# Six heads' inverse in a decoder layer: three heads' transposed inverse and level products moved to the other half of the partitions

## The reference

```
sa    = einsum('bhvk,bhk->bhv', state, -kk_t)
state = state * w_t + sa * (kk_t * a_t) + v_t * k_t
out_t = einsum('bhvk,bhk->bhv', state, r_t)
```

## Time and profile before

| | |
|---|---|
| median of three runs | 1374.96 us |
| the profiled execution's own time | 1372.77 us |
| its span, first to last instruction | 1370.7 us |
| PE busy over the span | 1268.2 us (93%) |
| DVE busy over the span | 511.4 us (37%) |
| mean granted TensorE clock | 0.971 |
| first start of line 692 (batch 0) | 373.0 us |
| starts of line 692 in batches 1 to 7 | 407.5, 443.6, 478.5, 514.5, 550.3, 586.6, 622.9 us |
| last start of line 739 (batch 7) | 657.8 us |

### The profile page before, as it was taken

The page is one execution under the profiler, slowest core; times in us unless marked ns, Lnnn a source line. Parts: engine busy times, 40 slices in busy tenths (PEclk is TensorE's granted clock), DMA queues, the critical chain, the costliest instruction groups (busy, mean ns, idle before and its releaser), DMA issues.

```text
span 1370.7 us, 23143 instructions
## 1 busy us (share of the span) xinstructions
PE 1268.2 (93%) x9642; PEld 628.1 (46%) x9642; DVE 511.4 (37%) x934; ACT 349.3 (25%) x482; POOL 108.1 (8%) x177
## 2 busy tenths in 40 slices
PE   7999999999999999999999964999999999999960
PEld 3444444444577777777445532333333333333320
DVE  3035310344178887886355355111111111110118
ACT  1044302234134433345221112111111111111114
POOL 1000000000111111010000001011101010101010
PEclk9999999999999999999999986999999999999985
DMA  5110010010000000001704008866789499397135
GB/s 215 42 35 31 31 46 31 31 31 16 0 3 3 33 3 34 3 3 37 289 1 156 31 16 339 305 237 223 251 308 316 153 319 375 90 383 226 31 74 217
DMA packets 61012, 170.17 MB, mean 124 GB/s; under 512 B 3184, under 2 KB 3312, under 8 KB 60928
## 3 DMA queue, kind: packets, MB, share of 16 engines
q1 hardware_dynamic: 54384, 145.31, 28.2%
q0 software_dynamic: 6544, 23.63, 7.1%
HBM read 144.29 MB, written 24.64 MB: 123 GB/s over the span
## 4 chain that ended last, share of the span: by engine, by line
PE 86%; DVE 5%; ACT 4%; DMA 2%; issue 2%; SPq 0%; POOL 0%; POOLq 0%; DVEq 0%; ACTq 0%
PE PS L1762 32%; PE PS L204 19%; PE PS L1251 8%; PE PS L643 6%; PE PS L213 3%; PE PS L954 2%; PE PS L966 2%; PE PS L976 2%; PE PS L1755 2%; PE PS L347 1%; PE PS L1391 1%; PE PS L739 1%; DMA XS<-in_xT 1%; ACT XS L999 1%; PE PS L692 1%
## 5 line engine op out<-in xcount | busy, mean ns | idle before, releaser
L204 PE MATMUL PS<-XS 128*128 128x512 f32 x672 | 294.5, 598 | 7.3 <-DMA XS<-in_xT 6.9
L1762 PE MATMUL PS<-XS,YT 128*64 128x512 f32 x656 | 287.6, 596 | 0.9 <-DVE YT L1843 0.9
L1762 PE MATMUL PS<-SQ,YT 128*64 128x512 f32 x488 | 216.0, 596 | 0.0
L1762 PE MATMUL PS<-RK,YT 128*64 128x512 f32 x672 | 211.1, 593 | 0.0
L204 PEld LDWEIGHTS PS<-XS 128*128 128x128 f32 x672 | 127.2, 191 | 172.8 <-issue 164.0
L1762 PEld LDWEIGHTS PS<-XS,YT 128*64 128x64 f32 x656 | 89.0, 138 | 183.0 <-issue 181.9
L1850 DVE TENSOR_TENSOR YT<-YT,PS 128x256 f32<-128x256 f32 x42 | 15.8, 417 | 271.8 <-PE PS L1762 271.8
L1251 PE MATMUL PS<-SQ,YT 128*128 128x512 f32 x256 | 114.0, 594 | 0.0
L643 PE MATMUL PS<-XS 64*64 64x64 f32 x2880 | 101.2, 221 | 4.4 <-ACT XS L782 2.6
L1762 PEld LDWEIGHTS PS<-RK,YT 128*64 128x64 f32 x672 | 65.9, 137 | 74.8 <-issue 74.8
L643 PEld LDWEIGHTS PS<-XS 64*64 64x64 f32 x2880 | 90.2, 135 | 21.4 <-issue 13.1
(11 more groups left out here) (375 smaller groups left out, 1519.0 us busy)
## 6 DMA issues: line engine op xcount, KB each, us to landing
RK<-in_w_down SPq DMA_DIRECT2D x6, 2048.0 KB, 13.2
XS<-in_w_in SPq DMA_DIRECT2D x21, 512.0 KB, 3.2
XS<-in_w_gate SPq DMA_DIRECT2D x5, 2048.0 KB, 13.5
XS<-in_w_upx SPq DMA_DIRECT2D x5, 2048.0 KB, 18.9
XS<-in_w_down SPq DMA_DIRECT2D x5, 2048.0 KB, 10.2
RK<-in_w_gate SPq DMA_DIRECT2D x5, 2048.0 KB, 20.3
SQ<-in_w_gate SPq DMA_DIRECT2D x4, 2048.0 KB, 21.4
RK<-in_w_upx SPq DMA_DIRECT2D x4, 2048.0 KB, 21.7
```

Source lines behind the costliest of these rows:

```text
L204: m = e.matmul(acc[:, half * HB:(half + 1) * HB], XS[:, 8 + n % 4, kt * P:(kt + 1) * P], XS[:, kt, half * HB:(half + 1) * HB], start=kt == ...
L1762: ins = e.matmul(acc[r, :], rows[:, r], third_cols(n, k, at, HB), start=start, stop=stop)
```

## The change

`T_` and the masked matrices stay as they are. For the heads 0 to 2 `U_` and `M1` now live in the other half of the partitions (chunk 0 in 64 to 127, chunk 1 in 0 to 63); for the heads 3 to 5 they stay. `QUARTERS` lists the twelve products in an order in which four successive ones have four different corners (r is the half of the chunk, q the half where `U_` and `M1` live), and `in_quarters` puts three heads in each PSUM bank. The level products, the corrections of `T_`, Z and WY go through all four corners. The corrections of `U_` read and write the half q and stay on the two diagonal corners, in the order q, other, other, q.

What must move with it: the first content of `U_` for the heads 0 to 3 comes from eight new products on PE (`start`, in two halves of four), written to PSUM, and DVE starts `U_` with two predicated copies instead of one, in the next part of its list. The key rows of heads 0 to 2 must lie in half q, so POOL makes a copy of the keys with the chunks swapped (`KS`, three copies) and transposes of g 0 and 1 read it. `rows(1)` and `rows(2)` move behind the corrections of the levels 1 and 3, and Z moves from level 1 to level 5. PSUM banks alternate between levels.

```
+                for g, h, to in ((0, slice(0, P), KS[:, 0, :]), (1, DIAG[0], KS[DIAG[0], 1, :])):
+                    ins = e.tensor_copy(to.rearrange("p (c t) -> p c t", c=2),
+                                        KB[h, g, tk].rearrange("p (c t) -> p c t", c=2)[:, ::-1, :])
+                ins.then_inc(s_ks, 1)
+                wait(e, s_ks, b + 1)
+                e.tensor_copy(KS[DIAG[1], 1, :], KB[DIAG[1], 1, tk]).then_inc(s_mo, 1)
+                wait(e, s_mo, b + 1)
...
+        QUARTERS = [(n // 2, DIAG[n % 2], n, c, DIAG[c], DIAG[c ^ (n < NPAIR)])
+                    for i in range(NPAIR) for n in (i, i + NPAIR) for c in range(2)]
+        def spread(acc):
+            return blocks(acc[:, :])[:, 0:16:3, :]
+        def in_quarters(e, acc, product):
+            for g, h, n, c, r, q in QUARTERS:
+                to, left, right = product(g, h, n, c, r, q)
+                ins = e.matmul(acc[to, 3 * n * C:(3 * n + 1) * C], left, right, start=True, stop=True)
+            return ins
         def level_product(e, b, lv):
             wait(e, s_tl, b * NTL + lv)
             if lv == 1:
                 wait(e, s_mk, 2 * (b + 1))
-            else:
-                wait(e, s_m1, b * NM1 + lv - 1)
-            same_chunk(e, RB(3), a1, of_t).then_inc(s_pm, 1)
+            in_quarters(e, PS[2 + lv % 2], lambda g, h, n, c, r, q: (q, BUF[r, g, KA + 1, h], block64(T_, r, n)))\
+                .then_inc(s_pm, 1)
+        def level_inverse(e, b, lv):
+            in_quarters(e, PS[3 - lv % 2], lambda g, h, n, c, r, q: (r, block64(U_, q, n), block64(M1, q, n)))\
+                .then_inc(s_pt, 1)
+        def level_transposed(e, b, lv):
+            for g, h, n, c, r, q in QUARTERS:
+                ins = e.matmul(block64(RB(2 * (lv % 2)), q, n), block64(M1, q, n), block64(U_, q, n),
+                               start=True, stop=True)
+            ins.then_inc(s_pu, 1)
...
+            def start(hh):
+                for g, h, n, c, r, q in QUARTERS:
+                    if n < 4 and n % 2 == hh:
+                        ins = e.matmul(block64(RB(1), q, n), KB[h, 3 + g, ck[c]], KB[h, g, ck[c]], start=True, stop=True)
+                return ins
...
             wait(e, s_mk, 2 * b + 1)
+            start(0).then_inc(s_px, 1)
             rows(0, 0)
-            rows(1, 1)
+            wait(e, s_px, 2 * b + 1)
+            start(1).then_inc(s_px, 1)
             level_product(e, b, 1)
-            wait(e, s_tok, 3 * b + 2)
-            rows(2, 1)
             yield
...
                 if lv < LEVELS - 1:
-                    same_chunk(e, RB(2), of_u, of_m1).then_inc(s_pt, 1)
-                same_chunk(e, RB(0), of_m1, of_u).then_inc(s_pu, 1)
-                if lv == 1:
-                    wait(e, s_tok, 3 * b + 3)
-                    same_chunk(e, RB(1), lambda r, g, h, n: BUF[r, g, KA + 3, h],
-                               lambda r, g, h, n: BUF[r, g, KV, h]).then_inc(s_pz, 1)
+                    wait(e, s_tok, 3 * b + (1, 2, 2, 3)[lv - 1])
+                    if lv == 3 and b > 0:
+                        wait(e, s_st, 2 * b - 1)
+                        wait(e, s_so, 2 * b - 1)
+                    level_inverse(e, b, lv)
+                else:
+                    wait(e, s_st, 2 * b)
+                    wait(e, s_so, 2 * b)
+                    in_quarters(e, PS[2], lambda g, h, n, c, r, q: (q, BUF[r, g, KA + 3, h], BUF[r, g, KV, h]))\
+                        .then_inc(s_pz, 1)
+                level_transposed(e, b, lv)
+                if lv in (1, 3):
+                    rows(lv // 2 + 1, 3)
...
-            for g, hh, h, n in HEADS:
-                for r in DIAG:
-                    ins = e.matmul(PS[3][r, n * P:(n + 1) * P], block64(U_, r, n), BUF[r, g, KZ:KK + 1, h],
-                                   start=True, stop=True)
+            for g, h, n, c, r, q in QUARTERS:
+                at = n // NPAIR * HB + n % NPAIR * P
+                ins = e.matmul(PS[3][r, at:at + P], block64(U_, q, n), BUF[q, g, KZ:KK + 1, h], start=True, stop=True)
             ins.then_inc(s_pw, 1)
...
+            yield
             wait(e, s_mk, 2 * (b + 1))
-            level(U_, upper, 0, BUF[:, :, KA + 1, :]).then_inc(s_ul, 1)
-            yield
+            level(U_[:, 4 * C:6 * C], upper, 0, blocks(BUF[:, 2, KA + 1, :]))
+            wait(e, s_px, 2 * (b + 1))
+            level(U_[:, 0:4 * C], upper, 0, blocks(RB(1)[:, 0:4 * C])).then_inc(s_ul, 1)
             yield
```

More of the change, by code:

```diff
@@ L637, in keep_clock @@
                 e.matmul(bank, identb[:, :], restart[:, 0:bank.shape[1]], start=True, stop=True)
-        def same_chunk(e, acc, left, right):
-            for g, hh, h, n in HEADS:
-                for r in DIAG:
-                    ins = e.matmul(block64(acc, r, n), left(r, g, h, n), right(r, g, h, n), start=True, stop=True)
-            return ins
-        a1 = lambda r, g, h, n: BUF[r, g, KA + 1, h]
-        of_t, of_u, of_m1 = [lambda r, g, h, n, x=x: block64(x, r, n) for x in (T_, U_, M1)]
+        QUARTERS = [(n // 2, DIAG[n % 2], n, c, DIAG[c], DIAG[c ^ (n < NPAIR)])
+                    for i in range(NPAIR) for n in (i, i + NPAIR) for c in range(2)]
+        blocks = lambda x: x.rearrange("p (n c) -> p n c", c=C)
+        def spread(acc):
[4 more added lines that the diff above has]
+                ins = e.matmul(acc[to, 3 * n * C:(3 * n + 1) * C], left, right, start=True, stop=True)
+            return ins
         def level_product(e, b, lv):
@@ L781, in level @@
                 wait(e, s_pm, b * NM1 + lv)
-                e.copy(M1, RB(3)[:, 0:NH * C]).then_inc(s_m1, 1)
+                e.copy(blocks(M1), spread(PS[2 + lv % 2])).then_inc(s_m1, 1)
             rows(0, 0)
-            rows(1, 1)
             level(1)
-            rows(2, 1)
             yield
-            wait(e, s_pz, b + 1)
-            e.copy(BUF[:, :, KZ, :], pairs3(RB(1)[:, 0:NH * C])).then_inc(s_zc, 1)
+            rows(1, 3)
             yield
@@ L793, in mats_act @@
                 yield
+                if lv == 3:
+                    rows(2, 3)
+                if lv == LEVELS - 1:
+                    wait(e, s_pz, b + 1)
+                    e.copy(BUF[:, :, KZ, :].rearrange("p g (h c) -> p g h c", h=2),
+                           spread(PS[2]).rearrange("p (g h) c -> p g h c", h=2)).then_inc(s_zc, 1)
                 yield
@@ L797, in mats_act @@
             wait(e, s_so, 2 * b)
-            e.copy(WY, PS[3][:, 0:NH * P]).then_inc(s_wy, 1)
+            e.copy(JG[:, :, :], PS[3][:, :].rearrange("p (c x) -> p c x", c=2)[:, :, 0:2 * GC]).then_inc(s_wy, 1)
             yield
@@ L807, in level @@
             def level(x, mask, lv, src):
-                return e.copy_predicated(pairs3(x), mask[:, lv:lv + 1, :].broadcast_to([P, NPAIR, P]), src)
+                x = blocks(x)
+                return e.copy_predicated(x, mask[:, lv:lv + 1, 0:C].broadcast_to(x.shape), src)
+            wait(e, s_init, b + 1)
+            wait(e, s_pq, b + 1)
             if b == 0:
                 e.memset(ST[:, 0, :], 0.0)
-            wait(e, s_init, b + 1)
-            wait(e, s_pq, b + 1)
             for hh in range(2):
@@ L829, in mats_dve @@
                     wait(e, s_pt, b * (NTL - 1) + lv)
-                    level(T_, lower, lv, pairs3(RB(2)[:, 0:NH * C])).then_inc(s_tl, 1)
+                    level(T_, lower, lv, spread(PS[3 - lv % 2])).then_inc(s_tl, 1)
                 wait(e, s_ul, b * NUL + lv)
                 wait(e, s_pu, b * (NUL - 1) + lv)
-                level(U_, upper, lv, pairs3(RB(0)[:, 0:NH * C])).then_inc(s_ul, 1)
+                level(U_, upper, lv, blocks(RB(2 * (lv % 2))[:, 0:NH * C])).then_inc(s_ul, 1)
                 if lv in (2, 4) and b > 0:
```

12 lines of the change are left out of this document (5 added, 7 removed).

## The result

The changed kernel takes 1356.88 us (median of 4 runs, 1355.1 to 1360.83), the kernel before 1375.17 us beside it (4 runs). The ratio is 0.9877, 95% interval 0.9849 to 0.9905: 18.3 us faster. The forecast was 1353 us, its working minus 20.5 us. The total is close, but that is partly luck: it is a sum of parts that were not all where I had put them, and the profiled execution, 1357.56 us against 1372.77, shows only 15.2 us of it.

The account below looks back on a forecast made before the run. PE was taken to set the pace, with DVE close behind. Savings of 16.2 us in six middle batches, 1.5 in batch 0 and 2.8 in batch 7 make 20.5 us off, forecast 1353 us, range 1344 to 1365.

Parts of the forecast that it names:

- Four corners, 3.5 us a batch: Level products, corrections of `T_` and Z: ten groups of 24 records, each 0.35 us instead of 0.70, 3.5 us off.
- the rival that rested on it: Chance 0.03: four corners don't help these products, 1379 us, or near 1371 by the skill page's 25 ns floor.
- WY 0.6 us: WY through four corners takes 0.86 us instead of 1.45 with its changeover, 0.6 us off a batch.
- `start` 0.47 us: Eight added products, 16 records at 29 ns, add 0.47 us of PE a batch; bounds 0.23 to 0.93.
- Sum on PE, 3.33 us: PE's savings less its added work in one batch: 3.33 us off, 26.6 us over eight batches.
- step 4: `rows(1)` and `rows(2)` stand in two more places between products of other shapes: 0.3 us on a batch.
- The wait of `rows(2)`: `rows(2)` no longer waits behind ACT's two copies: 1.6 us over all batches, 0.2 us a batch off.
- What does not arrive in a middle batch: DVE's lag keeps back 0.7 us and POOL's reads 0.1, leaving 2.7 us a middle batch, 16.2 over six.
- Batch 0, "cost there 0.8 us" for POOL: POOL's key copies, unhidden in batch 0, cost 0.8 us (bounds 0 and 1.9); the batch still gains 1.5 us.
- Batch 7, 2.8 us: Last batch gains 2.8 us: DVE has room, a norm's table load and square on ACT take 0.4 to 0.6.
- The corrections of `U_` kept their overlap: Denies a rival, chance 0.04: order q, other, other, q loses overlap, up to 3.5 us a batch, 1380 us.
- DVE did not become the bound: Denies a rival, chance 0.20: DVE's remaining waits make a batch 35.2 us, 10 us off in all, 1363 us.

Follow-up runs that it names:

- second run of the changed kernel: The changed kernel measured once more with nothing altered: 1356.74 us, ratio 0.9873 to the kernel before.
- POOL's order: Against the changed kernel, POOL sets `T_` and `U_` to the identity before the decayed keys and key copies in batch 0 alone: 1353.9 us, ratio 0.9852.

## Why the prediction was right, and where it was not

1. **Four corners, 3.5 us a batch: right.** 0.36 us first to last record for 0.697, ten times. These are 23 steps of 15.7 ns on the average; in the trace four starts stand 6 to 7 ns apart each time and the next four begin 58 ns after them (107 ns the first time). The Trainium skill ("TensorE: Matmul & The Clock Gate", "Wait — 56ns, not 53.3ns?") lets starts come no closer than about 25 ns; for products on different corners the trace does not agree, and the rival that rested on it fell. The order of issue matters otherwise than I thought: changed after twelve records it gives back half of the gain, after six more than all of it.
2. **WY 0.6 us: right**, 0.82 us for 1.45.
3. **`start` 0.47 us, the middle of wide bounds: right.** The first eight records take 0.23 us, 33 ns a step; the second eight run among the first level product's, and the two together take 0.58 us where a level product alone takes 0.36. With the changeover of the first half that is 0.60 us, inside the bounds of 0.23 to 0.93.
4. **Sum on PE, 3.33 us: right.** Six batches lost 17.3 us; PE's idle time in them went from 5.1 to 7.1 us, so its work lost 19.3 us, 3.2 a batch. The changeovers of step 4 were not measured by themselves.
5. **The wait of `rows(2)`: right.** No wait for ACT stands at line 735 any more.
6. **What does not arrive in a middle batch: mis-sized, and for the wrong reason.** I had 0.7 us for DVE and 0.1 for POOL's reads; 0.3 us was lost, and most of it to ACT. DVE's `U_` start is 0.30 + 0.44 us as forecast, but in these six batches PE waited for neither it nor the attention product. The test with less work for DVE moved nothing; the one with less for ACT moved 0.2 us a batch. So 2.9 us came for 2.7, a good number resting partly on a wrong step. PE's waits for DVE over all eight batches grew from 4.9 to 8.1 us, as the last paragraph of the prediction asked, but from the wait in batch 0 and small ones, not from the start of `U_`.
7. **Batch 0, "cost there 0.8 us" for POOL: the step that failed.** The copies take 0.93 us and, with 0.13 us for DVE's zeroing of the state, which the sum had left out, delay PE by 1.1 us, near the forecast. But with the wait grown to 2.96 us the granted clock fell for 10.2 us, and the batch took 3.1 us more instead of 1.5 less. The kernel before with these copies and the moved zeroing lost 3.7 us there. The prediction had no term for the clock. With the clock held by spare matmuls the batch is 33.9 us, 0.6 under before, so 0.9 us of the 1.5 is missing even then; PE's waits for ACT's copy in this batch grew from 1.3 to 2.2 us.
8. **Batch 7, 2.8 us: mis-sized by 1.1 to 2.7.** 41.2 us in the second run of the changed kernel and with POOL's order, 42.8 in the profile of the result, for 42.9 before. In the latter, 1.6 us of the miss is the clock (3.4 us at half speed). The rest is waiting that I had at 0.4 to 0.6 us: with the clock held PE's waits in this batch grew from 3.0 to 4.2 us. Before the first norm's sums PE waits 0.70 us for DVE's attention product, where I had given DVE room, and 0.81 us for ACT's square (line 1097), which stands behind a table load from 617.67 us; before, it waited 1.1 us at this place. Another 0.6 us is put down to issue, in front of a part of the output projection.
9. **The rivals.** The corrections of `U_` kept their overlap (0.648 us a group), and the four corners did help. DVE did not become the bound. Nothing behind the batches changed: from the first norm record to the end of the span it is 704.9 us before and 704.3 after.

In the profile, then, the middle batches gave 1.1 us more than forecast, batch 0 4.6 less and batch 7 2.7 less: 14.3 us by 651.5 us, for 20.5. The profiled executions differ by 15.2 us, the medians by 18.3: the profile of before was 2.4 us under its median, that of after 0.7 over, and it holds both lapses. The mean clock of the four executions of the result is 0.965 twice (the profiled one and 1360.83 us) and 0.968 twice (1356.19 and 1355.1 us), so two of them had some 8 us less at half clock (an estimate, 0.003 x 1356 us / 0.5); where in the span, no profile shows. That the median came so near to the forecast owes something to this.

## What to carry to other kernels

Small matmuls that use a 64 x 64 corner each should have their operands on four corners, and be issued so that the corner changes from one product to the next. Both count: a group took 0.36 us so, 0.52 us with the same operands and the pair of corners changed after twelve records, and 0.85 us with runs of six on one corner, which is more than the 0.70 us of two corners in turn. A new wait of PE at a place where it already waits is priced not by its length alone: look at the granted clock behind it, in more than one profile, and fill it. Ordering the work of the idle engine so that its first reader is served first shortens the wait, but in six of seven profiles the clock still fell. After PE gets faster, look for the copy that stands behind long work in another engine's list; here that, not the second busiest engine, is where part of the gain leaked (0.2 us of some 0.3 a batch).

## What was not expected of the hardware

- A corner starts a record of 64 columns each 58 ns (58.4 ns between its neighbours in a group); two corners in turn give 29, four 15 ns. Records for idle corners overtake waiting ones, but, as far as these durations tell, only over a short distance: 24 records took 0.36 us with the corner changed at every product, 0.52 us with the pair of corners changed after twelve records, and 0.85 us with the corner changed after six.
- The clock fell to the 1.2 GHz level in or behind a wait of 2.96 us (2.95 in the kernel before with added copies), and held behind one of 1.88 us. In batch 0 of seven kernels with nearly the same waits there, none longer than 1.6 us, it held in one profile and fell in six. Within the recurrence it stayed down for 3.4, 6.8 or 10.2 us at a time. Of two profiles of the same kernel with the same waits in batch 7, one shows a fall there and one none, so one profile tells neither that a wait is safe nor that it is not.
